# Block-sparse attention heads: the value matmuls of each head pair and kind gathered in the last of its three steps

## The reference

```python
ss = jnp.einsum('bqghd,bgqkld->bghqkl', qrg, k_sel) * scale
p_sel = softmax(where(valid_s, ss, NEG))
o_sel = jnp.einsum('bghqkl,bgqkld->bqghd', p_sel, v_sel)
...
sw = jnp.einsum('bqghd,bsgd->bghqs', qrg, k_w) * scale
p_w = softmax(where(valid_w, sw, NEG))
o_win = jnp.einsum('bghqs,bsgd->bqghd', p_w, v_w)
...
out = jnp.einsum('bsch,bschd->bshd', gates, o).reshape(b, s, NSA_HEADS * DH)
return out @ w_o
```

## Time and profile before

| what | value |
|---|---|
| median of 3 runs | 2097.75 us (2097.69 to 2097.76) |
| the profiled execution, its own time | 2098.55 us |
| its span in the trace | 2096.8 us |
| PE busy | 2078.5 us (99%) |
| DVE, ACT, POOL busy | 1520.8 us (73%), 989.0 us (47%), 717.2 us (34%) |
| mean granted clock of TensorE | 0.999 |

### The profile page before, as it was taken

One profiled execution on the slowest core, in us unless ns is written; L12 is line 12 of the kernel. 1 busy time (PEld: TensorE's weight loads), 2 busy tenths in 40 slices (PEclk: granted clock), 3 DMA queues, 4 the chain that ended last, 5 costly groups with the idle time before them and its releaser, 6 DMA issues.

```text
span 2096.8 us, 31979 instructions
## 1 busy us (share of the span) xinstructions
PE 2078.5 (99%) x12566; PEld 1749.0 (83%) x12566; DVE 1520.8 (73%) x2061; ACT 989.0 (47%) x1655; POOL 717.2 (34%) x588
## 2 busy tenths in 40 slices
PE   9999999999999999999999999999999999999998
PEld 6888688888999998777689999988975678899997
DVE  6866775658988886387768787766578757777774
ACT  4433564445544454355554333344537755334344
POOL 2301520027443434054463232301147646323221
PEclk9999999999999999999999999999999999999999
DMA  6233135223323333211133323233520022332321
GB/s 181 91 107 85 51 101 171 71 71 101 106 86 106 116 96 96 81 51 52 40 91 101 121 81 121 83 119 91 152 75 2 1 60 82 101 113 88 115 87 51
DMA packets 293303, 188.44 MB, mean 90 GB/s; under 512 B 9249, under 2 KB 287009, under 8 KB 293153
## 3 DMA queue, kind: packets, MB, share of 16 engines
q1 hardware_dynamic: 292864, 186.18, 29.7%
q10 hardware_dynamic: 288, 0.21, 0.1%
HBM read 183.48 MB, written 2.10 MB: 89 GB/s over the span
## 4 chain that ended last, share of the span: by engine, by line
PE 92%; DVE 4%; ACT 2%; issue 1%; DMA 0%; POOL 0%; ACTq 0%; SPq 0%; DVEq 0%
PE ps L542 90%; PE ps L576 2%; DVE wl L515 1%; ACT wh L505 1%; DVE sb_small L3478 0%; DMA p_xt<-in_x 0%; DVE ns_x L3524 0%; DVE ns_x L3523 0%; DVE tp_up L2330 0%; DVE H L679 0%; DVE nt_pts L3506 0%; DVE st_L L2735 0%; ACT XH L563 0%; DVE tp_up L675 0%; DVE tt_t L2071 0%
## 5 line engine op out<-in xcount | busy, mean ns | idle before, releaser
L515 DVE TENSOR_TENSOR wl<-raw,wh 128x1024 fp32r<-128x1024 f32 (+1 forms) x334 | 429.3, 1299 | 240.5 <-ACT wh L505 239.8
L542 PE MATMUL ps<-xb_x,wh 128*128 128x256 f32 (+1 forms) x1584 | 388.4, 336 | 1.4 <-DVE st_k L2780 0.6
L505 ACT CAST wh<-raw 128x1024 fp32r<-128x1024 f32 (+1 forms) x334 | 322.5, 981 | 132.1 <-PE ps L542 119.9
L542 PEld LDWEIGHTS ps<-xb_x,wh 128*128 128x128 f32 x1584 | 265.6, 188 | 31.1 <-DVE H L679 0.9
L542 PE MATMUL ps<-tt_t,wh 128*128 128x256 f32 x1536 | 277.4, 280 | 0.8 <-ACT tp_q L2257 0.3
L542 PE MATMUL ps<-xb_x,wl 128*128 128x256 f32 (+1 forms) x792 | 264.5, 334 | 0.0
L542 PEld LDWEIGHTS ps<-tt_t,wh 128*128 128x128 f32 x1536 | 237.0, 188 | 5.0 <-ACT tp_q L2257 1.2
L542 PE MATMUL ps<-XH,wh 128*128 128x512 f32 (+1 forms) x616 | 227.5, 369 | 1.2 <-DVE H L709 0.8
L542 PE MATMUL ps<-XH,wl 128*128 128x512 f32 (+1 forms) x616 | 222.5, 361 | 0.0
L542 PE MATMUL ps<-XL,wh 128*128 128x512 f32 (+1 forms) x616 | 222.0, 360 | 0.0
L542 PE MATMUL ps<-tt_t,wl 128*128 128x256 f32 x768 | 214.1, 279 | 0.0
(11 more groups left out here) (442 smaller groups left out, 4552.1 us busy)
## 6 DMA issues: line engine op xcount, KB each, us to landing
raw<-in_mlp_w SPq DMA_DIRECT2D x128, 512.0 KB, 4.0
raw<-in_w_gate_up SPq DMA_DIRECT2D x44, 512.0 KB, 3.9
raw<-in_w_in SPq DMA_DIRECT2D x28, 512.0 KB, 3.7
raw<-in_sb_w_qkv SPq DMA_DIRECT2D x24, 512.0 KB, 3.6
raw<-in_w_down SPq DMA_DIRECT2D x22, 512.0 KB, 5.8
raw<-in_w_out_mix SPq DMA_DIRECT2D x16, 512.0 KB, 3.6
raw<-in_w_kv SPq DMA_DIRECT2D x16, 512.0 KB, 3.8
raw<-in_nsa_w_kv SPq DMA_DIRECT2D x12, 512.0 KB, 3.8
```

What stands on the lines that cost most here:

```text
L505: e.copy(shaped(WH[i % NH], i), source(i)).then_inc(*w_hi.up(i))
L515: e.tensor_tensor(shaped(WL[i % NH], i), source(i), shaped(WH[i % NH], i).bitcast(F), ALU.subtract).then_inc(*w_lo.up(i))
L542: return e.matmul(out, a, b, start=start, stop=stop, skip_group_check=True)
```

## The change

The table `VALUES` goes away. Instead of spreading a group's four value calls over the three steps 3G + 6, 3G + 7 and 3G + 8 (one, one and two of them), all four are issued in the last of these. The calls themselves, their order among each other, their operands and what they wait for are the same, and no other engine's list is touched.

```diff
@@ -2917,7 +2917,6 @@
     TURNED_AT = {3: 0, 17: 1}
     MAX_AT = {4: 0, 7: 1}
     GATE_AT = {9: (1, 0), 11: (1, 1)}
-    VALUES = {0: (0,), 1: (1,), 2: (2, 3)}
 
     def query_unit(o):
         return "ng" if o == 8 else f"nq{o}"
@@ -3310,8 +3309,8 @@
                 pe_cmp_turn(e, TURN_AT[n])
             if n % 12 == 11:
                 pe_nsa_compressed(e, n // 6 - 1)
-            if n >= 6:
-                for j in VALUES[n % 3]:
+            if n >= 8 and n % 3 == 2:
+                for j in range(4):
                     pe_nsa_values(e, (n // 3 - 2) * 4 + j)
         pe_.end("heads_ns")
         for o in range(8):
```

## The result

The changed kernel takes 2111.9 us (median of 6 runs, 2111.07 to 2114.36) against 2097.76 us (6 runs, 2097.69 to 2097.90): ratio 1.007, 95% interval 1.006 to 1.008. It is slower by 14.2 us; 2109.1 us was forecast, in a range of 2103.0 to 2112.5.

What follows compares the result with a forecast made beforehand. TensorE was taken to set the 8.06 us period of a group. Terms +3.2 (banks), +6.2 (copy behind `out`), -0.3 (step 14), +1.1 (other VectorE work), +1.2 (tail) gave +11.4: 2109.1 us, range 2103.0 to 2112.5.

Steps and rivals of the forecast that it cites:

- the saving: On TensorE, four value calls in a row take 2.31 us against 2.61 spread: 0.30 less a group, 4.2 for 14 groups.
- Wait 1: Scores of a group's third step (C) wait for first step's (A) exponentials to free shared banks: C at A+4.12; net +3.2 us.
- Wait 2: Second half of third step's transposes waits for VectorE's copy behind `out`, until A+6.65 (from first step's scores): 6 times 1.03, +6.2 us.
- Other work between A and C: VectorE's compressed heads and last query's rotation may delay its copy in groups of steps 6, 9, 21: +1.1 us (0 to 3.1).
- The wait that step 14 already had: Step 14 already waited some 0.3 us for VectorE's late copy before the change, so -0.3 us in the sum.
- Tail: From step 45's transposes (T) to the projection, values of G=14 come after GpSimd's last scaling (T+4.15): T+9.09, +1.2 us.
- Only the banks' wait: Rival: VectorE's copy is in time, so only the wait for score banks and the end cost: +4.4, 2102.1 us; chance 0.08.
- the saving stays: Rival: exponentials and `out` come early enough to hide both waits, only the saved drains count: -4.2, 2093.6 us; chance 0.03.
- nothing happens: Rival: TensorE's work is the same and stalls fall into gaps that exist anyway: 2097.8 us; chance 0.04.
- The clock falls: Rival: new idle times bring TensorE from 2.4 to 1.2 GHz in places, about 8 us more: 2117 us; chance 0.05.

Runs made afterwards that it cites:

- the kernel with none, one and three calls: Against the changed kernel, a group's value calls split as none in its first step, one in its second, three in its third; 2101.41 us, ratio 1.0016.
- the kernel with the tail spread: Changed kernel, with only the values of G=14 spread over steps 48, 49 and 50 as before; 2111.14 us, ratio 1.0061.
- the values in step B: Against the changed kernel, all four value calls in the group's second step, the compressed heads' call one step forward; 2103.68 us, ratio 1.0027.

## Why the prediction was right, point by point

- **Which engine bounds, and the saving.** Right: four values in a row take 2.30 us (2.31 forecast), A's scores and transposes 1.99.
- **Wait 1.** Right: C at A+4.12 in the trace, A+4.12 forecast. A group with nothing else costs +0.24 to +0.27 us (0.23 forecast). Shown by its own release with wait 2 taken away, and by its absence when one value call stands between A and C.
- **Wait 2.** Right in place and cause: A+6.65 as forecast. The price was 0.1 too low: over the +0.25 of a plain group it is 1.12 us, not 1.03, since half of C's transposes takes 0.48 us when it starts from a wait (1654.72-1654.24), where I had used half of the undisturbed 0.74. Moving `out` took 6.7 us out of the stage (140.85 to 134.14); 6.2 was forecast for the term.
- **Other work between A and C.** Mis-sized: 1.1 us taken, with 0 to 3.1 as bounds. Over a plain group, the groups of steps 6, 9 and 21 cost 0.6, 0.4 and 0.8 us, 1.8 together, and that of step 27, which I had left out, 0.35. In the last two GpSimd's scaling ran 2.73 and 2.28 us in place of 1.90, and the second half of the transposes started 0.11 and 0.12 us behind its end. In step 27 it alone was late (copy over at 1644.33, load at 1644.81). In step 21 the copy, behind the rotation, was as late: over at 1625.58, the scaling at 1625.59, the load at 1625.70. Why the scaling took longer is not shown. GpSimd was named as "in time", 0.24 us ahead, of which the 0.11 us from its end to the load must still go off. So thin a margin should have been a bounded term.
- **The wait that step 14 already had.** -0.3 forecast; the group of step 12 is 0.48 us cheaper than the other ones with `out`.
- **Tail.** +1.2 forecast; from the transposes of step 45 to the projection it is 9.20 us (9.09 forecast) against 7.92. GpSimd's last scaling is over at T+4.15, as forecast, and the weight loads of the last half of the transposes start at T+4.26 (their matmuls at 1707.18 below):

```profile
1702.88 1.09 PE L576 MATMUL ps<-cst,ne_e 128*128 128x128 f32 x8
...
1705.13 1.90 POOL L3497 TENSOR_TENSOR ne_t<-ne_t,sb_small 128x128 f32<-128x128 f32 x4 [2.38 <-DVE sb_small L3486]
...
1707.18 0.52 PE L576 MATMUL ps<-cst,ne_t 128*128 128x128 f32 x3 [0.41 <-POOL ne_t L3497]
1707.62 0.20 PEld L542 LDWEIGHTS ps<-nt_pts,ns_vs 128*64 128x64 f32 x4 [0.17 <-issue]
```

- **Sum.** The stage is +13.2 us, not +11.4: +1.1 from the other work, +0.5 from wait 2, +0.3 from wait 1, +0.1 from the tail, -0.2 from step 14. The 0.6 us ahead of the stage are of the trace before: its stage starts at 1553.29, that of all nine other traces between 1552.44 and 1552.85, and its execution was 0.8 us above the median of its kernel. The median of six has another 0.8 us, since three of the six executions are among the long ones. So the measured median is above the upper bound of the sum (2111.2), and only what the range had beyond that took it in. A fourth long execution among the six would have put it at the edge of the range or outside: that it is inside is partly luck.
- **The rivals.** "Only the banks' wait", "the saving stays" and "nothing happens" are refuted by the trace. "The clock falls", priced at 8 us and given 0.05, is no rival but an addition that comes in some executions, at 1.6 us a time where a trace shows it: last section.

Two rules of the Trainium skill stood beside the forecast's sum. The drain between tiling modes (TensorEngine Tiling (Array Packing), Key Properties) agrees with what is saved, 0.15 us a switch, and is in no conflict with the loss; no run here tells the drain from other costs of a switch. "Consistent bubbles" can mean too little PSUM for the next tile (Perfetto Trace Analysis, Optimization Strategy): the row at A+4.12 is one, though no run here gave the scores more banks. The larger bubble at A+6.65 hangs on a single bank per head for the transposes; it closed by moving `out`, without any more PSUM.

## What to carry to other kernels

Work of the bounding engine that is spread between two uses of one buffer is slack for the other engines: before gathering it, list for each pair of pieces that share a buffer, or of which one feeds the other by way of another engine, the distance that they need (release minus start, from the timeline) and the distance that is left. Gathering gains at most 0.15 us for each saved switch here (0.09 in the kernel with none, one and three calls), and loses whatever any one of these distances falls short, in every round. Price also the engines that "are in time" by a few tenths, and look at the end of the loop by itself, where no further scores fill the waits.

## What the runs showed of the hardware that was not expected

Waits of TensorE of 0.4 and 0.9 us in one group, in a stage where its longest idle time had been 0.42 us, stood ahead of a fall of its clock for a few microseconds, in some groups only. Stretches of the kernel with the tail spread, its group of step 24 (columns: busy us of PE, PEld, DVE, ACT, POOL, then the granted clock, DMA share, GB/s):

```profile
1632.00:1634.00 2.00, 1.57 (x20) 1.28 (x20) 0.85 (x4) 2.00 (x6) 1.32 (x4) 1.00 0.00 0
1634.00:1636.00 2.00, 1.10 (x12) 0.73 (x9) 1.97 (x7) 0.69 (x4) 0.58 (x2) 1.00 0.00 0
1636.00:1638.00 2.00, 2.00 (x7) 0.69 (x8) 1.97 (x9) 1.86 (x10) 1.86 (x2) 0.54 0.00 0
1638.00:1640.00 2.00, 2.00 (x12) 0.83 (x10) 0.20 (x1) 0.88 (x5) 1.79 (x3) 0.61 0.00 0
```

TensorE was busy for 1.57 and 1.10 of 2 us, with idle times of its own of 0.43 and 0.90 us, then the clock fell from 2.4 to 1.2 GHz (0.54 and 0.61 are means over stretches that hold some of both), and the four value calls took 3.83 us in place of 2.30:

```profile
1635.85 0.31 PEld L576 LDWEIGHTS ps<-cst,tmp 128*128 128x128 f32 x3 [1.13 <-DVE nt_pts L3504]
1636.44 0.30 PEld L542 LDWEIGHTS ps<-nt_pts,ns_vs 128*64 128x64 f32 x4 [0.28 <-issue]
...
1640.27 0.19 PEld L542 LDWEIGHTS ps<-nk_kwh,xb_x 64*128 64x128 f32 x2 [0.17 <-issue]
```

The group took 11.07 us in place of 9.43. The same happened once with the values in step B: there the group of step 12 took 11.21 us, behind waits of 0.6 and 1.4 us of the load engine, with the values at half clock again (0.50 from 1595 to 1598 us). Other executions of both kernels were shorter by about as much: 2110.01 against the profiled 2111.14, and 2103.35 to 2103.76 against the profiled 2105.00. The same two waits in five other groups of the trace above, and in the two traces of the changed kernel, left the clock alone. So at this size the waits alone don't decide it, and what else does is not shown. That the long executions of the changed kernel are this too is likely: they lie 1.4 to 3.6 us above the others, about one or two such falls of 1.6 us, and their mean granted clock is the lowest of all. Where in them the clock fell was not shown, for lack of a trace. With `out` moved, where the larger wait is gone, six executions lay within 0.8 us. The Trainium skill describes a clock gate that goes by how busy the array has been (TensorE: Matmul & The Clock Gate, Part 1); the rows agree with that as far as they go: the clock fell behind stretches in which TensorE was busy for a smaller share, and equal stretches elsewhere left it up.
